# mLSTM states and normalizers moved between the tiles of the output projection, the last expert scatter handed over bank by bank, and the final norm taken on turned rows

## What is computed

```
# mLSTM, layer 1 (8 heads, dk 128, dv 256), both directions
C_new = decay * C + einsum('bsh,bshv,bshd->bhvd', ws, vc, kc)     # output state C
n_new = decay * n + einsum('bsh,bshd->bhd', ws, kc)               # output state n
hsum = head_rmsnorm(hf + flip(hb), norm_g)
y = (o * hsum) @ w_out                                            # 2048 -> 1024
# every layer
xc = xc + gc2 * moe(hc2, ...)                                     # residual after the experts
# the end
y_prompt = rmsnorm(xc, final_g)
y_sample = rmsnorm(xl, final_g)
```

## Time and profile before

| | |
|---|---|
| median of 3 runs | 1867.9 us (1867.45 to 1869.59) |
| profiled execution, its own time | 1866.5 us |
| its span in the trace | 1864.7 us |
| mean granted TensorE clock | 0.974 of 2.4 GHz |
| PE busy | 1771.1 us, 95% of the span |
| DVE, ACT busy | 476.1 us, 385.3 us |
| end of the mLSTM layer (first head product to the projection's first matmul) | 670.60 to 724.84 us |
| output projection of the mLSTM layer | 724.84 to 780.88 us |
| last residual of the program to the end of the span | 1844.91 to 1864.7 us |

### The profile page before, as it was taken

The page is one execution under the profiler, slowest core; times in us unless marked ns, Lnnn a source line. Parts: engine busy times, 40 slices in busy tenths (PEclk is TensorE's granted clock), DMA queues, the critical chain, the costliest instruction groups (busy, mean ns, idle before and its releaser), DMA issues.

```text
span 1864.7 us, 21714 instructions
## 1 busy us (share of the span) xinstructions
PE 1771.1 (95%) x8838; PEld 1034.5 (55%) x8838; DVE 476.1 (26%) x1240; ACT 385.3 (21%) x774; POOL 40.6 (2%) x52
## 2 busy tenths in 40 slices
PE   4999999999999988999999999999999999999996
PEld 2677544446745867854444747864444687544444
DVE  1242511115300242241111244350111252411112
ACT  1232200003102472110001232320000342200002
POOL 1000000000000000000000000000000000000000
PEclk9999999999998988999999999989999999899998
DMA  9979699997998225379999895869999819699992
GB/s 323 365 284 387 261 422 427 427 418 275 354 368 300 99 105 202 140 286 428 427 426 415 313 332 208 328 243 424 427 427 422 311 67 383 250 423 426 427 426 96
DMA packets 134407, 609.47 MB, mean 327 GB/s; under 512 B 12486, under 2 KB 19278, under 8 KB 109473
## 3 DMA queue, kind: packets, MB, share of 16 engines
q1 hardware_dynamic: 117264, 589.32, 79.4%
q10 hardware_dynamic: 12528, 10.70, 1.8%
q0 software_dynamic: 4512, 8.02, 1.1%
HBM read 606.15 MB, written 8.92 MB: 330 GB/s over the span
## 4 chain that ended last, share of the span: by engine, by line
PE 87%; DVE 4%; DMA 3%; ACT 3%; issue 1%; ACTq 1%; DVEq 0%; SPq 0%; POOLq 0%
PE PS L1535 23%; PE PS L961 22%; PE PS L1546 12%; PE PS L1499 7%; PE PS L991 4%; PE PS L1043 3%; PE PS L1011 2%; DVE arena L2085 2%; DMA ring<-in_moe_wg 1%; PE PS L1540 1%; PE PS L1479 1%; DMA ring<-in_w_mod 1%; PE PS L1029 1%; DVE RS L1696 1%; PE PS L1521 1%
## 5 line engine op out<-in xcount | busy, mean ns | idle before, releaser
L1535 PE MATMUL PS<-ring,arena 128*64 128x512 f32 x1280 | 375.5, 601 | 1.6 <-DMA ring<-in_moe_wg 1.5
L893 ACT ACTIVATE arena<-PS 128x512 f32<-128x512 f32 (+1 forms) x130 | 70.6, 543 | 797.7 <-PE PS L1526 349.9
L1535 PEld LDWEIGHTS PS<-ring,arena 128*64 128x64 f32 x1280 | 116.9, 138 | 179.2 <-issue 179.1
L2085 DVE TENSOR_TENSOR arena<-arena,PS 128x512 f32<-128x512 f32 x32 | 33.5, 1046 | 638.9 <-PE PS L1535 638.9
L961 PE MATMUL PS<-HS,ring 128*128 128x256 f32 x768 | 176.6, 388 | 3.0 <-DVE HS L1788 1.7
L1535 PE MATMUL PS<-arena 128*64 128x512 f32 x576 | 169.6, 594 | 0.0
L961 PEld LDWEIGHTS PS<-HS,ring 128*128 128x128 f32 x768 | 147.0, 194 | 30.2 <-issue 8.6
L1499 PE MATMUL PS<-arena 128*128 128x256 f32 (+3 forms) x688 | 144.6, 361 | 5.1 <-ACT arena L893 3.7
L961 PE MATMUL PS<-arena,ring 128*128 128x256 f32 x640 | 140.1, 381 | 2.5 <-ACT arena L659 1.1
L1546 PE MATMUL PS<-ring,arena 128*64 128x512 f32 x640 | 141.7, 595 | 0.0
L1499 PEld LDWEIGHTS PS<-arena 128*128 128x128 f32 (+1 forms) x688 | 112.2, 190 | 44.2 <-issue 22.7
(11 more groups left out here) (341 smaller groups left out, 1711.9 us busy)
## 6 DMA issues: line engine op xcount, KB each, us to landing
ring<-in_w_mod SPq DMA_DIRECT2D x48, 2048.0 KB, 15.7
ring<-in_moe_wu SPq DMA_DIRECT2D x41, 2048.0 KB, 21.0
ring<-in_moe_wd SPq DMA_DIRECT2D x41, 2048.0 KB, 21.6
ring<-in_moe_wg SPq DMA_DIRECT2D x41, 2048.0 KB, 20.3
arena<-in_moe_wg SPq DMA_DIRECT2D x24, 2048.0 KB, 18.1
HS<-in_moe_wu SPq DMA_DIRECT2D x12, 2048.0 KB, 18.3
arena<-in_moe_wu SPq DMA_DIRECT2D x12, 2048.0 KB, 20.3
arena<-in_moe_wd SPq DMA_DIRECT2D x12, 2048.0 KB, 24.9
```

Of the source, the lines that this page charges most:

```text
L893: A(dst, src, func).then_inc(S(sem), 1)
L1535: ins = mm(PS[64 * e:64 * e + 64, b, :], XG[:, k, 64 * e:64 * e + 64], w[:, k], start=(k == 0), stop=(k == KD - 1))
L2085: tt(by_k(HID), row(SG), row(bank(here[1])), ALU.mult).then_inc(S("hid"), 1)
```

## The change

PE and ACT in the mLSTM layer: all eight states move out of the way of the heads, to places behind single groups of the projection (0 to 3 behind the groups of `c=0, r=1`, 4 to 7 behind those of `c=1, r=0`). The normalizers become 8 matmuls of 256 columns that leave the 8 heads on 8 partitions, behind the group `c=1, r=1, m=0`; their transpose and one copy go. `turn_z(1)` moves behind the second group. The heads take three pairs of banks in turn instead of two. ACT has no state before the last `scaled`, its order of `lead`, `first`, `second`, `turned` and `root` is another, and the transfers of `m` are issued before the heads. The upper half of `mHN` gets a place of its own, since the states still need `mKW`. In the experts the last scatter steps its semaphore after each bank, and `residual` waits bank by bank. At the end `X` itself is transposed, ACT sums squares along rows (`YSS`), a root and a reciprocal of 128x2 follow, and DVE multiplies bank, reciprocal and a copy of `final_g` on all partitions (`FG`) in one instruction for each of 4 banks. One load of `final_g` leaves the start of the program.

```diff
@@ experts' tail, PE and DVE
-                def scatter(par, sem, first=False, ts=range(8)):
+                def scatter(par, sem=None, first=False, ts=range(8)):
                     for t in ts:
                         ins = pick(bank(t // 2, N2 * (t % 2), N2 * (t % 2) + N2), YS[:, P * t:P * t + P], WTS[:, par, 0:N2],
                                    first and t % 2 == 0, True)
-                    if t == 7:
-                        ins.then_inc(S(sem), 1)
+                        if sem and t % 2:
+                            ins.then_inc(S(sem), 1)
...
-                v.wait_ge(S("scatter"), n0 + 8)
                 v.wait_ge(S("x_scatter"), before + nx)
-                residual(None, 0, l, 5, lambda m: bank(m // 2, N2 * (m % 2), N2 * (m % 2) + N2))
+                residual("scatter", 4 * l, l, 5, lambda m: bank(m // 2, N2 * (m % 2), N2 * (m % 2) + N2), each=2)
@@ mLSTM, PE
-                    b = 2 * (h % 2)
+                    b = (0, 2, 6)[h % 3]
...
-                head(0)
-                head(1)
                 for h in range(4):
-                    state(h)
-                head(2)
-                head(3)
+                    head(h)
                 turn(2)
                 turn(3)
                 for h in range(4, MH):
                     head(h)
-                pe.wait_ge(S("l_c_sb"), 4)
+                pe.wait_ge(S("l_z1"), 6)
+                pe.wait_ge(S("l_z1a"), 6)
                 turn_z(0)
                 pe.wait_ge(S("l_z1"), MH)
                 pe.wait_ge(S("l_z1a"), MH)
-                for h in range(4, MH):
-                    state(h)
-                for d in range(2):
-                    for h in range(MH):
-                        ins = mm(bank(2, 8 * d + h, 8 * d + h + 1), mKW[:, h, d], ones[:, 0:1], start=True, stop=True)
-                ins.then_inc(S("l_n"), 1)
-                turn_z(1)
-                after(pe, "l_n_sb")
-                tp(PS[0:16, 2, 128:256], mNS, ident).then_inc(S("l_nT"), 1)
-                after(pe, "l_nT_sb")
-                pe.wait_ge(S("l_c_sb"), MH)
...
                                     pe.wait_ge(S("l_hn"), 8)
+                                elif m == 2:
+                                    turn_z(1)
...
+                            if c == 0 and r == 1:
+                                state(m)
+                            if c == 1 and r == 0:
+                                state(4 + m)
+                            if c == 1 and r == 1 and m == 0:
+                                pe.wait_ge(S("l_c_sb"), 5)
+                                for h in range(MH):
+                                    ins = mm(PS[0:8, 4, 0:N2], c_("win")[:, 40 - h:48 - h], mKW[:, h].rearrange("p a b -> p (a b)"), start=(h == 0), stop=(h == MH - 1))
+                                ins.then_inc(S("l_n"), 1)
@@ mLSTM, DVE
                 hidden(0)
+                join(1)
                 hidden(1)
-                join(1)
                 hidden(2)
                 hidden(3)
+                hidden(4)
+                hidden(5)
                 scale(0)
-                for h in range(4, MH):
-                    hidden(h)
+                hidden(6)
+                hidden(7)
                 gated(0)
@@ final norm: ACT, PE, DVE, SP
+            for j, (s, c) in enumerate(((0, 0), (1, 0), (0, 1), (1, 1))):
+                act.wait_ge(S("yT"), 2 * c + s + 1)
+                run(A(SQ[:, 0:2].rearrange("p a b -> p (a b)"), bank(4 + 2 * s + c), ACT.Square, accum_out=YSS[:, s, c:c + 1]), f"y_sq{j}")
+            after(act, "y_sum")
+            run(A(YR, YSS[:, :, 0], ACT.Sqrt, bias=c_("eps"), scale=1.0 / D), "y_root")
...
-            sumsq(2 * DEPTH)
-            for c in range(2):
-                pe.wait_ge(S("h0"), KD * 2 * DEPTH + 4 * c + 4)
+            for k in range(KD):
+                pe.wait_ge(S("x"), KD * 2 * DEPTH + k + 1)
                 for s in range(2):
-                    for k in range(4 * c, 4 * c + 4):
-                        ins = tp(bank(2 * s + c, P * (k % 4), P * (k % 4) + P), H[:, k, T * s:T * s + T], ident)
-                    ins.then_inc(S("yT"), 1)
+                    ins = tp(bank(4 + 2 * s + k // 4, P * (k % 4), P * (k % 4) + P), X[:, k, T * s:T * s + T], ident)
+                    if k % 4 == 3:
+                        ins.then_inc(S("yT"), 1)
...
+            for s in range(2):
+                for c in range(2):
+                    run(stt(XR[:, s, 512 * c:512 * c + 512], bank(4 + 2 * s + c), YR[:, s:s + 1], FG[:, 512 * c:512 * c + 512], ALU.mult, ALU.mult), "y_sb")
...
+            sp.dma_start(FG, I["final_g"].partition_broadcast(P)).then_inc(S("load_b"), 16)
+            for s, y in enumerate(("y_prompt", "y_sample")):
+                sp.wait_ge(S("y_sb"), 2 * s + 2)
+                sp.dma_start(O[y][0], XR[:, s]).then_inc(S("out"), 16)
```

More of the change, by code:

```diff
@@ L747, in first @@
                     act.wait_ge(S("l_h"), h + 1)
-                    run(A(mZ[1][:, h], bank(1 + 2 * (h % 2), 0, MDV), ACT.Copy, scale=mSCR[:, h:h + 1]), "l_z1a")
+                    run(A(mZ[1][:, h], bank((1, 3, 7)[h % 3], 0, MDV), ACT.Copy, scale=mSCR[:, h:h + 1]), "l_z1a")
                 def second(h):
@@ L1573, in pair @@
                             pe.wait_ge(S("ys"), 2 * n)
[L1574 removed]
+                            scatter(1 - par, first=(i == 1), ts=range(6))
                     if more and not first:
@@ L1579, in pair @@
                     if not first:
-                        scatter(1 - par, "scatter", first=(i == 1), ts=range(6, 8))
+                        scatter(1 - par, first=(i == 1), ts=range(6, 8))
                     if more:
```

106 lines of the change are left out of this document (51 added, 55 removed).

## The result

| | median | runs |
|---|---|---|
| before, beside it | 1868.74 us | 4 runs, 1867.45 to 1870.73 |
| the changed kernel | 1850.82 us | 4 runs, 1846.71 to 1852.83 |
| forecast | 1844.6 us | 1838.0 to 1851.5 |

The change makes the kernel faster by 1%: ratio 0.9901, 95% interval 0.9882 to 0.9919, some 18 us. The forecast was 6.2 us too low, and the measured median lies at the upper end of its range. The profiled execution took 1852.83 us, its span 1851.0, against 1866.5 and 1864.7 before.

The account below looks back on a forecast made before the run. PE, busy 95% of the span, was taken as the bound. Terms 12.6 (mLSTM) + 4.5 (experts' tails) + 5.9 (end) + 0.3 (start) = 23.3 us, giving 1844.6 us against the median of 1867.9; range 1838 to 1851.5.

Parts of the forecast that it names:

- mLSTM, forecast 12.6: End of the mLSTM layer: projection starts near 697 and ends at 768 to 768.5 instead of 780.9, 12.6 us less.
- the restart: Projection's start behind a pause of some 6 us: it begins at the lower clock, 2.0 us added.
- Experts' tails, forecast 3 x 1.5: Experts' end in layers 0 to 2: the bank-wise handover saves 1.5 us each, 4.5 in all (2.1 to 6.3).
- the floor that the text worked out as 2.1: Experts' tail: PE's scatter end plus eight sums gives 1029.8 against 1031.9, a gain of 2.1 us.
- PE, too, reads two registers and branches: Experts' tail, before the sums: PE's price not visible; with ACT's 1.49 us the gain would be 0.7.
- End of the program, forecast 5.9: Final norm and output on transposed X: the end comes at 1858.8, 5.9 us less (5.0 to 7.0).
- the four products: End of the program: DVE's products of 512 columns, between 0.48 and 0.97 us each, taken as 0.78.
- Start, forecast 0.3: Program start: one small ACT load of 0.41 us issue goes, 0.3 us less (0 to 0.6).
- The table load's drain: ACT in mLSTM: the skill's 1.38 us per table switch would make the gain 11.2 instead of 12.6.
- The low clock in the projection: Rival, mLSTM projection: low clock for some 17 us costs 8.5 instead of 2, time 1851.1; chance 0.08.
- The waits for weights of the experts: Rival, layer 1's experts: weights come late and eat up to 12.6 us, time 1857; chance 0.05.
- The handover without effect: Rival, experts' tails: table load and branches set the squares' start, 4.5 us less gain, time 1849; chance 0.07.

Follow-up runs that it names:

- e4_pad36: The changed kernel with 36 empty instructions in PE's pause ahead of the projection, which never reached the program, so a repetition of the changed kernel; 1846.53 us, ratio 0.9893.
- g2_states_mm9: The mLSTM part alone, with 9 one-column matmuls added in PE's pause ahead of the projection; 1857.23 us, ratio 0.9935.
- e2_scatter: The kernel of before with only the experts' bank-by-bank scatter handover changed; 1861.06 us, ratio 0.9965.
- f2_mm9: The changed kernel with 9 unread one-column matmuls (36 instructions) added in PE's pause ahead of the projection; 1843.55 us, ratio 0.9875.
- g3_nop36: The changed kernel with 36 instructions that only raise an unread semaphore, ahead of the projection; 1842.43 us, ratio 0.9851.
- h1_n_split: g1_n_nop36 with its 36 padding instructions split, 18 ahead of the last four heads and 18 ahead of the normalizers; 1839.37 us, ratio 0.9834.
- g1_n_nop36: The changed kernel with the normalizers moved into the pause ahead of the projection and 36 semaphore instructions as padding in one place; 1843.72 us, ratio 0.9874.
- f3_n_mm18: f1_mm18 with the eight normalizer matmuls moved from the projection's end into the pause ahead of it; 1847.45 us, ratio 0.9882.
- e1_states: The kernel of before with the mLSTM part alone, without the scatter handover and the new end; 1863.99 us, ratio 0.9989.
- f1_mm18: The changed kernel with 18 unread one-column matmuls (72 instructions) added in PE's pause ahead of the projection; 1849.93 us, ratio 0.9901.
- f4_mm82: f2_mm9 with 82 one-column matmuls instead of 9 ahead of the projection, 328 instructions more than the changed kernel; 1874.29 us, ratio 1.0033.

## Why the prediction was right, and where it was off

- **mLSTM, forecast 12.6: 12.44 against the profiled execution.** The start of the projection, its end, the eight states together, the normalizers and the restart all came within 1 us, and `turn_z(1)` and the last heads lie where the text put them. But the size was read off an execution with 17 us at half clock in the very stage; against the two other executions of the old stage it is 8.3 to 8.8 (10.4 to 10.9 with e4_pad36 for the changed kernel, 9.3 to 9.9 in g2_states_mm9). That forecast and result agree to 0.2 us is luck: both were read against the same execution of before. The costs of 3.78 for two states and 6.83 for the one-column matmuls were prices at half clock: the latter take 3.94 us in e2_scatter, at 0.92. The earlier trace rows showed that the clock was low; I took it as what this kernel does and not as what one execution did.
- **Experts' tails, forecast 3 x 1.5.** Two layers gained 2.26 and 2.18, the floor that the text worked out as 2.1; "PE, too, reads two registers and branches" costs nothing visible where the code is there. Layer 1 lost 3.8. This is the step that failed: I costed the branch as an instruction, from ACT's 1.49, and did not ask what the instructions behind it are read from. Nothing in the three parts touches this; the mLSTM part only moved the code. The sum of the tails is 0.7 instead of 4.5, and the traces of f2_mm9 and g3_nop36 show that 5.8 us come back with 36 instructions (13.11 to 7.27).
- **End of the program, forecast 5.9: 6.6.** From the last tile's end to the last product 5.9 us against 6.0 forecast, the four products 3.11 against 4 x 0.78. The rest is the last transfer: 3.05 us from issue to the span's end, where I took 3.6 to 4.0 from before. The first output was under way earlier, so less stood in front of the second.
- **Start, forecast 0.3: nothing.** The first norm's sums start at 42.36 in the changed kernel, at 42.30 before. The small load was covered.
- **The table load's drain** that the Trainium skill adds ("ScalarE: Activation LUTs", section "What ACT_TABLE_LOAD costs") stays unseen: in the changed kernel the dummy starts at 1013.88 behind a load from 1012.58 of 1.28 us, and the first square 0.23 later.
- **Two slips of the working**, on which nothing hangs: from 724.84 to 697 it is 27.8 us and not 27.5, and 2.1 less 1.49 is 0.6 and not 0.7.
- **Rivals.** The low clock in the projection lasted for 5 us of it and not 17. The waits for weights of the experts are 1.1 us longer than before, not 12.6. The handover without effect is refuted by e2_scatter. With the measured sizes and no stall in layer 1 the forecast's 23.3 would be 4.4 + 2.2 + 6.6 and 8.3 to 10.9 for the mLSTM part, 21.5 to 24.1 us; with the stall it is 6.0 less, 15.5 to 18.1. The 17.9 of the medians lie in it. That the time fell into the range although one tail went the other way is due to the width of the range: its upper end stood for two other mishaps, the low clock and the handover without effect.

Of the 6.0 us lost between the two profiled spans in unchanged stages, the longer time at 1.2 GHz (80 us instead of 70) covers up to 4 by an estimate from the normalizers, which take 6.06 us at the low clock and 3.62 at the high one; the rest is spread over waits for expert weights and for indices and was not taken apart. Why the clock is low for longer in one execution than in the next stays open as well. That PE's blocks of code are not asked for across a branch that has yet to be decided is read from the starts in the table and not shown by itself. That the position of the code decides is shown, and that PE stands on its branch meanwhile.

## What to carry to other kernels

When a change removes or adds instructions on an engine whose program has branches, look behind every branch for idle time that waits on nothing ("issue"), and compare the number of instructions on the page; if a stall has appeared, some instructions of padding in a place where the engine waits anyway move it away, and the next branch must be looked at too. A price read at a clock of 0.50 is a price of that execution: before it goes into a sum, see the same stage in a second trace. And a pause ahead of a long row of matmuls costs twice, once as idle time and once as the slow start behind it; independent work that fits into it can give back both, as in h1_n_split. Where it came too late or was too much, as in g1_n_nop36 and f3_n_mm18, it pushed the row back and little or nothing was gained.

## What the runs showed of the hardware

- TensorE's branch behind layer 1's last scatter took 6.19 to 6.25 us in the three kernels whose code behind mLSTM lies alike (changed kernel, e1_states, e4_pad36) and 0.32 to 0.33 in the others. It cost 4.0 to 4.1 us of standing and 1.76 us of slower records behind it (5.38 instead of 3.62 for 16, at a granted clock of 0.68). What is read as a border of a block inside a row of matmuls shortly behind a branch cost 1.8 to 2.0 us (f1_mm18, f3_n_mm18, f4_mm82).
- A matmul of 128x1 in 32 bit, which is two loads and two products in the trace, took 0.25 us at a granted clock of 0.92 (3.94 for 16 in e2_scatter) and 0.41 over the 82 in a row of f4_mm82, 33.3 us in all, with a mean granted clock of 0.53 though PE was never idle. The clock fell 2 us into that row and came back 3 us behind its end.
- Instructions that only raise a semaphore start 0.15 us apart on TensorE (g1_n_nop36, g3_nop36, h1_n_split), where I expected 0.08. The 36 empty ones without a semaphore of e4_pad36 are not in the program: 21622 instructions with and without them.
